# Products of the identity in TensorE's pauses: three before the output product, five at each norm, eleven at the layer norm

## What is computed

```
layer 0: p = modulate(rms_norm(h)) @ mix_in_w
         y = concat(diff_attention(p), rwkv7(p)) @ mix_out_w     # the output product
         h = h + gate * y
         h = h + gate * (relu(modulate(rms_norm(h)) @ w1)**2 @ w2)
layer 1: u = glu(modulate(rms_norm(h)) @ pw1_w + b)
         u = depthwise_conv31(u) + b
         y = silu(layer_norm(u)) @ pw2_w + pw2_b                  # the layer norm
         h = h + gate * y
         h = h + gate * (relu(modulate(rms_norm(h)) @ w1)**2 @ w2)
```

## Time and profile before

| | |
|---|---|
| median of 3 runs | 3244.95 us (3244.55 to 3248.17) |
| the profiled execution's own time | 3245.74 us |
| its span, first to last instruction | 3244.1 us |
| TensorE busy | 3021.5 us (93%) |
| VectorE busy | 2202.5 us (68%) |
| ScalarE busy | 1244.9 us (38%) |
| mean granted TensorE clock | 0.973 of full |

### The profile page before, as it was taken

One profiled execution on the slowest core, in us unless ns is written; L12 is line 12 of the kernel. 1 busy time (PEld: TensorE's weight loads), 2 busy tenths in 40 slices (PEclk: granted clock), 3 DMA queues, 4 the chain that ended last, 5 costly groups with the idle time before them and its releaser, 6 DMA issues.

```text
span 3244.1 us, 49985 instructions
## 1 busy us (share of the span) xinstructions
PE 3021.5 (93%) x20896; PEld 2496.8 (77%) x20896; DVE 2202.5 (68%) x2736; ACT 1244.9 (38%) x1430; POOL 217.1 (7%) x394
## 2 busy tenths in 40 slices
PE   5899999778889888999999999999889999999999
PEld 2588987536677766788888888799867888888887
DVE  3677766477887885577777878759974555555554
ACT  1322221174444443344443434343643343434342
POOL 1000000001000000012122121100000000000000
PEclk9799999899999998999999999999989999999999
DMA  9976887790000033668888888756205455555553
GB/s 326 352 273 238 317 289 246 271 368 24 12 14 13 22 67 106 208 230 285 279 295 281 293 292 277 260 166 184 92 23 181 159 194 186 191 185 192 194 182 130
DMA packets 306013, 640.59 MB, mean 197 GB/s; under 512 B 19035, under 2 KB 23937, under 8 KB 303585
## 3 DMA queue, kind: packets, MB, share of 16 engines
q1 hardware_dynamic: 269280, 529.94, 48.3%
q0 software_dynamic: 28384, 94.76, 9.0%
q10 hardware_dynamic: 8128, 12.72, 1.1%
HBM read 623.81 MB, written 13.40 MB: 196 GB/s over the span
## 4 chain that ended last, share of the span: by engine, by line
PE 83%; DVE 9%; DMA 4%; issue 2%; ACT 2%; ACTq 0%; SPq 0%; POOLq 0%; DVEq 0%
PE ps L445 46%; PE ps L463 15%; PE ps L465 7%; DMA raw<-in_ada_w_dram 3%; PE ps L2385 2%; PE ps L1662 2%; DVE rw_scl L1336 1%; DVE rw_mb L1353 1%; PE ps L382 1%; PE ps L1820 1%; PE ps L1772 1%; DVE rw_mt L1356 1%; DVE rw_scc L1339 1%; PE ps L1569 1%; DVE line L752 1%
## 5 line engine op out<-in xcount | busy, mean ns | idle before, releaser
L422 DVE TENSOR_TENSOR split_lo<-raw,split_hi 128x2048 fp32r<-128x2048 f32 (+1 forms) x372 | 849.7, 2285 | 496.7 <-ACT split_hi L410 488.8
L410 ACT ACTIVATE split_hi<-raw 128x2048 fp32r<-128x2048 f32 x368 | 702.1, 1911 | 1180.4 <-PE ps L445 840.3
L463 PE MATMUL ps<-xa,split_hi 128*128 128x512 f32 x2048 | 723.4, 398 | 6.4 <-ACT xa L617 6.4
L465 PE MATMUL ps<-xa,split_lo 128*128 128x256 f32 x2048 | 574.0, 280 | 0.0
L463 PEld LDWEIGHTS ps<-xa,split_hi 128*128 128x128 f32 x2048 | 384.6, 188 | 103.0 <-ACT xa L617 7.4
L445 PE MATMUL ps<-split_hi,hT_hi 128*128 128x512 f32 x1024 | 399.6, 390 | 0.0
L445 PE MATMUL ps<-split_hi,hT_lo 128*128 128x512 f32 x1024 | 398.5, 389 | 0.0
L445 PE MATMUL ps<-split_lo,hT_hi 128*128 128x512 f32 x1024 | 398.4, 389 | 0.0
L465 PEld LDWEIGHTS ps<-xa,split_lo 128*128 128x128 f32 x2048 | 386.5, 189 | 0.2
L445 PEld LDWEIGHTS ps<-split_hi,hT_hi 128*128 128x128 f32 x1024 | 192.2, 188 | 41.4 <-issue 1.8
L445 PEld LDWEIGHTS ps<-split_hi,hT_lo 128*128 128x128 f32 x1024 | 192.2, 188 | 40.2
(11 more groups left out here) (386 smaller groups left out, 4521.1 us busy)
## 6 DMA issues: line engine op xcount, KB each, us to landing
raw<-in_mlp_w_dram SPq DMA_DIRECT2D x256, 1024.0 KB, 5.4
raw<-in_ada_w_dram SPq DMA_DIRECT2D x64, 1024.0 KB, 9.6
raw<-in_mix_in_w_dram SPq DMA_DIRECT2D x48, 1024.0 KB, 5.7
raw<-in_conv_pw_w_dram SPq DMA_DIRECT2D x48, 1024.0 KB, 5.4
gate<-in_ada_w_dram SPq DMA_DIRECT2D x172, 256.0 KB, 5.0
line<-in_ada_w_dram POOLq DMA_DIRECT2D x171, 256.0 KB, 5.1
late<-in_ada_w_dram POOLq DMA_DIRECT2D x85, 256.0 KB, 5.0
tmpa<-in_ada_w_dram SPq DMA_DIRECT2D x84, 256.0 KB, 4.9
```

The lines of the kernel that those rows point to most:

```text
L410: nc.scalar.activation(split_hi[:, c, :, 0:n], raw[:, c, :, 0:n], ACT.Copy).then_inc(hi_done, 1)
L422: nc.vector.tensor_tensor(split_lo[:, c, :, 0:n], raw[:, c, :, 0:n], split_hi[:, c, :, 0:n], ALU.subtract).then_inc(lo_done, 1)
L463: pe.matmul(ps[:, base + j, :], split_hi[:, c, kk, j * P:(j + 1) * P], both, start=(k == 0), stop=False, skip_group_check=True)
L465: mm = pe.matmul(ps[:, base + j, 0:SEQ], split_lo[:, c, kk, j * P:(j + 1) * P], xa_hi[:, k, :], start=False, stop=(k == KT - 1), skip_grou ...
```

## The change

A function keep_clock is added. It issues n products of the identity with the identity repeated four times (128x128 by 128x512, f32, two passes each) into a bank of PSUM whose content nobody reads at that time; they wait for nothing and increment no semaphore. Nothing is removed or moved. It is called with 3 ahead of TensorE's third stage_end, with 5 ahead of each norm's wait for rdiag, and with 11 between the layer norm's variance sums and the wait for the bias rows.

```diff
+        def keep_clock(pe, bank, n):
+
+            wide = ident[:, :].rearrange("p (a n) -> p a n", a=1).to_broadcast([P, 4, P])
+            for _ in range(n):
+                pe.matmul(ps[:, bank, :].rearrange("p (a n) -> p a n", a=4), ident[:, :], wide, start=True, stop=True)
+
         def pe_rest(pe):
+            keep_clock(pe, 7, 3)
             stage_end(pe, 3)
             pe.wait_ge(rws["y"], HEADS + 1)
...
             def norm(q, tr0):
+                keep_clock(pe, 5, 5)
                 pe.wait_ge(norm_xn, q + 1)
                 pe.wait_ge(res_ps, (4, 20, 24)[q - 1])
                 pe_scaled_turns(pe, tr0, 0, 4)
...
             mm.then_inc(var_ps2, 1)
+            keep_clock(pe, 5, 11)
             pe.wait_ge(rest_in, 16 + 64)
```

## The result

The changed kernel's median is 3255.41 us over 7 runs (3250.79 to 3260.98), against 3244.55 us (3241.39 to 3248.17) for the kernel before, over 7 runs on the same chip: 10.9 us more. The ratio is 1.003, with a 95% interval of 1.002 to 1.004. It is slower, by 0.3%. The forecast was 3252.2 us with a range up to 3258.0, so the time lies inside, 3.2 us above the forecast. The profiled execution has an own time of 3254.40 us and a span of 3252.7; both are 8.7 us more than before.

A forecast was written before the change was run, and what follows sets the result against it. TensorE alone was taken to set the pace in the MLPs. Terms 3.6 + 0 + 4.8 - 1.0 gave +7.4 us, 3253.1 for the profiled execution; against the median, 3252.2 us, range 3245.0 to 3258.0.

The forecast's parts named there:

- The barrier: Output product: three products ahead of stage_end(3) hold the barrier; cost 3.6 us, bounds 1.5 and 4.1; slow start stays.
- The norms: Five products at each norm: faster turns gain nothing, slowed first products cost 1.6 us each, 4.8 in all.
- the pause grows to 3.7 us, a length that the clock doesn't survive: Norms: idle before the first product grows from 1.62 to 3.7 us, and the clock probably falls.
- The layer norm: Eleven products behind the variance: a third of the 2.8 us gain taken, -1.0 us; bounds 0 and 2.8.
- The argument against the gain: Layer norm: clock fell 0.6 us after the bias passes; one-row passes seem like idle time, making the pause 4.1 us.
- The sum: Whole kernel: 3.6 + 0 + 4.8 - 1.0 = +7.4 us on the profiled execution; +7.2 us against the median.
- the forecast case: Whole kernel: barrier late, norms at a moderate price; +4.5 to +10 us, 3249.5 to 3255; chance 0.50.
- the third rival: Norms slow for 5 to 5.9 us each; +10.8 to +12 us in all, about 3257; chance 0.14.
- The rule weighed: TensorE's pauses: advice to leave no idle gaps; judged unmet, since each filler leaves a 2 to 5 us pause.
- The first rival: Barrier not held, clock stays up at output product and layer norm; -4.8 us, 3240.1; chance 0.07.

The follow-up runs named there:

- e8: Six products ahead of stage_end(3), none elsewhere, against the kernel before: 3251.76 us against 3245.13, ratio 1.0019.
- e4: Only three products, behind stage_end(3) instead of ahead of it, against the kernel before: 3242.83 us against 3246.22, ratio 0.9989.
- e5: Five products at each norm plus four right behind the first turns, none elsewhere, against the kernel before: 3248.16 us against 3245.13, ratio 1.0004.
- e11: Two products at each norm in place of five, none elsewhere, against the kernel before: 3247.37 us against 3245.08, ratio 1.0007.
- e2: Only the five products at each norm, against the kernel before: 3251.95 us against 3246.22, ratio 1.0011.
- e3: Only the eleven products at the layer norm, against the kernel before: 3247.32 us against 3246.22, ratio 1.0.
- e12: Only eleven products at the layer norm, behind the one-row bias passes instead of ahead, against the kernel before: 3245.39 us against 3247.02, ratio 0.9999.
- e6: Eleven products at the layer norm and two more behind the bias passes, none elsewhere, against the kernel before: 3245.12 us against 3245.13, ratio 0.9996.
- e7: Three products behind stage_end(3), eleven plus two at the layer norm, none at the norms, against the kernel before: 3238.63 us against 3245.13, ratio 0.9974.
- e9: Three products behind stage_end(3), eleven plus two at the layer norm, nine ahead of the convolution, against the kernel before: 3239.63 us against 3245.08, ratio 0.9985.
- e1: Only the three products ahead of stage_end(3), against the kernel before: 3248.78 us against 3246.22, ratio 1.0006.

## Why the prediction was right, and where it wasn't

**The barrier** was right in mechanism and size: forecast 3.6 us, measured 3.61 and 3.71; L2038 released by TensorE at 1271.2, forecast 1270.9; the start of the product still slow, 10 passes in 4.1 us. e8 and e4 show that it is the barrier: the cost grows with the work ahead of it, and turns into the gain of 2.0 us behind it.

**The norms** came out at 1.6, 1.35 and 1.7 us in the changed kernel's profile, 4.7 in all for a forecast of 4.8, and at 7.57 us from turns to product, as said. e5 shows the cause, since a filled pause takes the cost away. But the step "the pause grows to 3.7 us, a length that the clock doesn't survive" was too simple: in e11 and at e2's norm 3 the same price was paid behind 2.10 us, and e11 lived through 3.80. In the changed kernel and e2 all six chunks were slow, for 3.4 us each as forecast, with pauses of 3.7 us in five of them. The size held better than its reason, and in part by luck: the reason would have told nothing about e11.

**The layer norm** is the term that failed. The prediction put -1.0 us (bounds 0 and -2.8), which is where its sum was off; the changed kernel and e3 gave nothing. The argument against the gain, the clock falling 0.6 us after the one-row passes, stood in the prediction and deserved more weight: with the eleven products the clock fell 1.6 us after them (changed kernel) and 0.4 us after them (e3). Products behind the one-row passes brought back part (e12) and then all (e6) of the 2.8 us. e6 also cut the pause to 0.3 us, so it doesn't tell the height of the passes from the length of the pause, and e12 does so with one execution only. The traces together say more. Ahead of the norms, where full-height passes come last, the clock fell 2.0 to 5.0 us after them (the 30 pauses without products). At the layer norm, with the one-row passes last, it fell 0.2 to 3.2 us after those, which is 2.1 to 5.2 us after the last full-height pass (nine executions). So here the 2.0 us of one-row passes did no more for the clock than idle time.

**The sum** was +7.4 us for the profiled pair, which measured +8.7. The 1.3 between them is the layer norm's 1.0 and 0.4 of small stretches, less 0.1 at the norms. It was luck that the pair could be cut so cleanly: the part ahead of L1404's end, which no edit touches, ends within 0.14 us in the two, but anywhere from 1261.1 to 1271.0 us over all the executions. The medians differ by 10.9 us, 2.2 more than the pair. The parts alone give 2.6 + 5.7 + 1.1 = 9.4 by their medians and 8.4 by their traces, the medians with about 3 us of uncertainty on each. The median of 3255.41 is also just above the forecast case's own 3249.5 to 3255, and nearer to the third rival's 3257 than to the forecast. The traces speak against that rival: all eight slow chunks behind a norm that were profiled (the changed kernel, e2, e11) lost 1.35 to 1.65 us, with slow stretches of 3.4 us, and none of 5 to 6. Whether its price was paid in executions without a trace stays open.

**The rule weighed**, to leave TensorE no long idle gaps between bursts (the Trainium skill, TensorE: Matmul & The Clock Gate, Why this matters for your kernels), agrees with e4, e6 and e7: where the fill reached up to the restart, 2.0 and 2.75 us came back in their traces. The first rival, which followed it, fell because the changed kernel's fills didn't reach that far, or stood ahead of a barrier.

## What to carry to other kernels

Work put into an engine's idle time is free only if it ends before whatever next waits for the whole engine: a drain and a barrier make the others wait for it as much as for real work, and the same fill belongs on the other side. A fill pays if it ends right at the restart and the work behind the pause was slow before; look at the first pass of the dense work (0.47 or 0.77 us here), and leave a pause alone that already ends fast. Filling or speeding up work ahead of a second pause can make that pause the expensive one.

## What the runs showed that wasn't expected

- The clock can fall where TensorE is busy without a break: in e9 it fell 1.3 us after four one-row passes with no idle time at all, and in e3 0.4 us after them, with no idle time until their end. But between pw2's dense blocks such a group cost the clock once in 42 times, so one-row passes alone don't bring it down. That fits the idle stretches of 0.9 to 2.2 us ahead of the norms' first products, all of which the clock outlived at the 30 norms without products.
- A pause's length doesn't decide alone. The clock outlived 3.80 us (e11, until 1.3 us into the turns) and was lost behind 2.10 us (e11, e2), 3.4 us after it had risen, but it outlived 2.16 us at e1's norm 2. The pause of 2.41 us ahead of the variance passes was lost in 6 executions of 14, though its instructions are the same in all. So one trace in which a pause is outlived doesn't tell that it will be in the next.
- Executions of the same instructions differ by 1.2 to 1.6 us in each MLP (722.8 and 721.4 us for the layer 0 stretch, with no added product near it), at the full granted clock. Which of the two comes showed no tie to any edit. With this, the variance passes' 1.5 to 1.7 us and a first part that ends anywhere between 1261.1 and 1271.0 us, a term of 2 us is seen in a trace cut at fixed instructions and hardly in a median.
